# In two up stages a load of up weights is issued ahead of a load of conditioning weights, and the multiplications of the first two conditioning blocks stand in other places

## The reference, cut to what matters

```
e = silu(c @ cond_w + cond_b)
for i in range(2):
    mod = e @ ada_w[i] + ada_b[i]                 # [1024] @ [1024, 6144]
    sh1, sc1, g1, sh2, sc2, g2 = split(mod, 6)
    y = mixer[i](x * (1 + sc1) + sh1)
    x = layer_norm(ALPHA * x + (1 + g1) * y)
    gate, up = split((x * (1 + sc2) + sh2) @ ffn_up[i], 2)    # [512, 1024] @ [1024, 5632]
    y = (silu(causal_conv(gate, taps) + bias) * up) @ ffn_down[i]
    x = layer_norm(ALPHA * x + (1 + g2) * y)
# the second kind: the same pattern, with silu(c_2) @ w_ada_2 [1024] @ [1024, 6144]
```

## Time and profile before

| what | value |
|---|---|
| median of 3 runs | 2812.2 us (2811.16 to 2816.44) |
| the profiled execution, its own time | 2816.42 us |
| its span in the profile | 2814.6 us |
| mean granted clock of PE | 0.985 |
| PE busy | 2681.7 us (95%) |
| PE weight load busy | 2020.7 us (72%) |
| DVE busy | 1686.3 us (60%) |
| ACT busy | 681.3 us (24%) |
| POOL busy | 166.3 us (6%) |
| loads of the ring from the conditioning weights | 33 of 2048 KB, median 7.7 us to landing |
| loads of the ring from the up weights | 33 of 2048 KB, median 7.7 us to landing |

### The profile page before, as it was taken

One profiled execution on the slowest core, in us unless ns is written; L12 is line 12 of the kernel. 1 busy time (PEld: TensorE's weight loads), 2 busy tenths in 40 slices (PEclk: granted clock), 3 DMA queues, 4 the chain that ended last, 5 costly groups with the idle time before them and its releaser, 6 DMA issues. The chain is left out here.

```text
span 2814.6 us, 30369 instructions
## 1 busy us (share of the span) xinstructions
PE 2681.7 (95%) x11908; PEld 2020.7 (72%) x11908; DVE 1686.3 (60%) x2960; ACT 681.3 (24%) x1292; POOL 166.3 (6%) x126
## 2 busy tenths in 40 slices
PE   5999999899999999999999999998999899999999
PEld 5466666658888888888887888884445454788888
DVE  4466666557777555554657777645476483666652
ACT  0333333221111021112102111104353362322200
POOL 0001000010000011000001000001232000000000
PEclk9999999999999999999999999999999999999999
DMA  7112211214443422112122444331011300222121
GB/s 326 41 60 90 90 60 60 90 60 153 160 166 131 157 96 91 65 64 90 64 73 88 169 158 171 142 112 64 30 76 60 149 2 31 83 78 82 69 103 51
DMA packets 24493, 275.02 MB, mean 98 GB/s; under 512 B 3480, under 2 KB 4376, under 8 KB 7072
## 3 DMA queue, kind: packets, MB, share of 16 engines
q1 hardware_dynamic: 19440, 266.45, 25.4%
q10 hardware_dynamic: 4912, 6.63, 0.7%
HBM read 270.97 MB, written 2.10 MB: 97 GB/s over the span
## 5 line engine op out<-in xcount | busy, mean ns | idle before, releaser
L384 PE MATMUL bank<-HT,ring 128*128 128x256 f32 x1056 | 253.9, 387 | 9.9 <-ACT HT L794 7.4
L1102 PE MATMUL bank<-HT,ring 128*128 128x512 f32 x512 | 250.8, 599 | 5.7 <-ACT arena L1370 5.7
L384 PE MATMUL bank<-arena 128*128 128x256 f32 x1056 | 249.5, 379 | 0.0
L384 PE MATMUL bank<-arena,ring 128*128 128x256 f32 x1056 | 249.5, 379 | 0.0
L384 PEld LDWEIGHTS bank<-HT,ring 128*128 128x128 f32 x1056 | 203.7, 194 | 46.2 <-issue 15.5
L384 PEld LDWEIGHTS bank<-arena 128*128 128x128 f32 x1056 | 200.6, 190 | 27.3
L384 PEld LDWEIGHTS bank<-arena,ring 128*128 128x128 f32 x1056 | 200.6, 190 | 27.3
L466 PE MATMUL bank<-arena,ring 128*128 128x256 f32 x936 | 210.5, 384 | 8.3 <-ACT arena L538 5.6
L466 PEld LDWEIGHTS bank<-arena,ring 128*128 128x128 f32 x936 | 179.4, 192 | 36.7 <-ACT arena L538 6.8
L1030 ACT ACTIVATE arena<-bank,ffc 128x512 f32<-128x512 f32 x66 | 51.3, 777 | 498.0 <-DVE bank L942 498.0
L2368 PE MATMUL bank<-HT,ring 128*128 128x512 f32 x320 | 146.0, 593 | 3.0 <-ACT HT L834 3.0
(11 more groups left out here) (462 smaller groups left out, 4387.2 us busy)
## 6 DMA issues: line engine op xcount, KB each, us to landing
ring<-w_ada SPq DMA_DIRECT2D x33, 2048.0 KB, 7.7
ring<-w_up SPq DMA_DIRECT2D x33, 2048.0 KB, 7.7
ring<-w_down SPq DMA_DIRECT2D x24, 1408.0 KB, 6.0
ring<-w_gdn SPq DMA_DIRECT2D x8, 2048.0 KB, 8.4
ring<-w_ret_qk SPq DMA_DIRECT2D x4, 2048.0 KB, 7.8
ring<-w_ret_v SPq DMA_DIRECT2D x4, 2048.0 KB, 7.6
ring<-w_ret_g SPq DMA_DIRECT2D x4, 2048.0 KB, 7.7
ring<-w_ret_out SPq DMA_DIRECT2D x4, 2048.0 KB, 7.7
```

Of the source, the lines that this page charges most:

```text
L384: last = nc.tensor.matmul(out_, w[:, k, :], x[:, k, :], start=(first and k == 0), stop=(k == 3), skip_group_check=not first)
L1102: last = nc.tensor.matmul(B[u % 2][:, :], w[:, u, k, :], HT[:, k, :], start=(k == 0), stop=(k == KC - 1))
```

## The change

Two things change in up stages 0 and 1, and nothing in up 2. In SP's list the third load of up weights (`("up", i, 2)`) is issued ahead of block 1 of the conditioning weights. The slots stay as they were, and so does what each load waits for: the up load for DVE's last multiplication of block 0, block 1 for PE's last product with the first up load. And the first two blocks are multiplied in other steps:

| step | place | before: block, slices | after |
|---|---|---|---|
| 0 | round 0, behind t | 0: 0, 1 | 0: 0, 1 |
| 1 | round 1, ahead of t | 0: 2, 3 | 0: 2, 3, 4 |
| 2 | round 1, behind t | 0: 4, 5 | 0: 5, 6, 7 |
| 3 | round 2, ahead of t | 0: 6, 7 | none |
| 4 | round 2, behind t | 1: 0, 1 | none |
| 5 | round 3, ahead of t | 1: 2, 3 | none |
| 6 | round 3, behind t | 1: 4, 5 | 1: 0, 1, 2, 3 |
| 7 | round 4, ahead of t | 1: 6, 7 | 1: 4, 5, 6, 7 |

From step 8 on all is as before.

```diff
             def ada(j, half):

+                first_blocks = {1: (0, 0, 2), 2: (0, 2, 5), 3: (0, 5, 8), 7: (1, 0, 4), 8: (1, 4, 8)}
                 step = 2 * j + half - 1
-                if i < 2 and 0 <= step < 40:
+                if i < 2 and step < 8:
+                    if step + 1 in first_blocks:
+                        dve_ada(dve, i + 1, *first_blocks[step + 1])
+                elif i < 2 and step < 40:
                     l, k = step // 4, 2 * (step % 4)
                     dve_ada(dve, i + 1, l, k, k + 2)
@@
         def _(sp):

-            for n, key in enumerate(loads):
+            issued = list(range(len(loads)))
+            for i in range(2):
+                n = load_at[("ada", i + 1, 1)]
+                issued[n:n + 2] = [load_at[("up", i, 2)], n]
+            for n in issued:
+                key = loads[n]
```

## The result

Predicted were 2797.5 us (2793.5 to 2804.0); measured are 2799.5 us as the median of four runs (2794.5 to 2800.7), against 2811.7 for the kernel before (four runs too; the 2812.2 of the table are the median of the first three of them). The ratio is 0.9946, 95% interval 0.9934 to 0.9958. A second group of runs gave 2800.7 against 2815.1, ratio 0.9949 (0.9936 to 0.9961). The kernel is faster, by 12 to 15 us: 12.2 and 14.4 by the medians of the two groups, 15.2 and 14.4 by the ratios.

The account below looks back on a forecast made before the run. PE was taken to wait in round 3 of two up stages for DVE, held by a late weight load, then run at low clock. Losses 8.08 and 8.46 us, less 0.92 each, save 14.7: 2812.2 to 2797.5 us (2793.5 to 2804).

Parts of the forecast that it names:

- The late load: First up stage: third up-weight load issued 6.1 us earlier, so PE's last product of round 3 starts 4.40 us earlier.
- The cost at M3(1): PE's last product of round 1: an added multiplication ahead of it leaves PE 0.92 us behind its free run.
- The pair of loads: Third up load and block 1's go out together: the first lands unslowed, about 7.5 us, the second 12.4 us after issue.
- Rival A: The paired loads share the engines, so the third up load lands late, at 660.3; about 2803 us, 10%.
- Block 1 in two fours: Rounds 3 and 4: block 1's multiplications stay hidden; the later fourth up load leaves 0.3 us cover in round 5.
- Rival B: Round 5: the fourth up load comes late because block 1 moved toward it; 0.5 to 1 us per stage, 2799, 15%.
- Rival C: Behind t(3): DVE stands waiting for block 1's load, delaying round 4; slower, 2816 us if it lands after 24 us, 3%.
- Rival D: PE's gap is taken up elsewhere in the stage, so time ends within 3 us of the old; 2811, 3%.
- The clock: Low PE clock behind the round-3 gap goes with the gap; 2.18 us of the second up stage's 8.46.
- The sum: First and second up stages save 7.16 and 7.54 us, together 14.7, with nothing given back later.

Follow-up runs that it names:

- That experiment: The changed kernel with the list of loads put back as before, so only the multiplications moved: 2806.5 us, ratio to before 0.9972.
- the second profile of the changed kernel: The changed kernel run once more without edits, in another group beside the kernel before: 2800.7 us against 2815.1.
- the gap filled: The kernel before with four unread matmuls added on PE in round 3 of both up stages, ahead of the wait for t(3): 2809.6 us, ratio 0.9987.

## Why the prediction was right

*The late load.* Right (though the wait of 4.4 us that the prediction sets out from stands in the second up stage; in the first, whose timelines it reads, it is 3.41): issue 11.8 us behind M3(0) (11.7 worked out), landing after 7.6 us, no wait at line 895, M3(3) set by PE alone.

*The cost at M3(1).* Right in kind, 0.97 us behind the free run where 0.92 was put. The clock was 1.00 over 640 to 650 us, with the gap of 0.81 us in it, and 1.00 over 1524 to 1530 us in the second up stage.

*The pair of loads.* 7.6 and 12.1 us against 7.7 and 12.4 taken from the start of the program; 7.7 and 13.4 in the second up stage. Rival A is refuted: the first of a pair wasn't slowed here (7.6 and 7.7 us, where the third up load, not one of a pair, took 7.5 and 8.5 before), and each of these pairs landed in the order of its issue. So did the pairs in the other order: 7.5 us for block 1 and 12.1 for the up load, 7.6 and 13.3 in the second up stage. That experiment shows the order to be worth 2.8 and 4.5 us a stage.

*Block 1 in two fours.* Right, and its cover even thinner than said: line 895 of round 5 waits 2.98 us, t(5) starts at 681.46 and M3(5) at 682.12, which with 0.47 us for the hand-over leaves 0.2 us where 0.3 was put. PE pays nothing there; in the second profile of the changed kernel, second stage, it pays 0.06 us (12.15 us from M3(4) to M3(5)). So Rival B, at 0.5 to 1 us, did not come in the changed kernel, but did where the loads stood in the old order (0.77 us at M3(5)).

*Rival C, slower by a blocking load.* It did not come, and its mechanism is real: 12.26 us at one multiplication with the list alone changed, slower than before.

*Rival D, hidden anyway.* It did not come: behind M3(5) of the first stage the distance to M3(0) of the second is 832.9 us before and 832.8 after, so nothing of the gain was given back.

*The clock.* Right. The 8.08 us of the first stage are the 5.34 by which M3(3) is late and 2.74 of low clock: M3(3) and the product behind it take 6.19 us (667.07 to 673.26) where two products take 3.45 (2 x 1.73), and the granted clock is 0.50 of full over 667 to 671 us and 1.00 over 673.26 to 675. With the gap filled they take 3.55 us at a clock of 1.00 in both stages: 4.7 us won against 4.9.

*The sum.* 14.7 us was predicted, 14.3 measured in the stages. What is missing is 0.05 us at M3(1), 0.10 at M3(2) and 0.03 at M3(3) in each stage: I had let t(2) and PE's own run tie at 654.0, and a tie still cost 0.10 us (8.74 for 8.64). By medians the saving was 12.2 us in the first group and 14.4 in the second. The difference of 2.0 us to the predicted time is within what runs of one kernel differ by (2794.5 us with a mean clock of 0.990, 2800.7 with 0.987), and of such a difference the last section shows 6 us ahead of the first up stage.

## What to carry to other kernels

In a ring with an ordered queue of loads, as this kernel's, a load goes out when its slot is free and its place in the queue has come (17.8 us behind M3(0) with its place alone moved, 11.8 with both). Moving only its place did harm here (9.7 us), and moving only the work that frees the slot gave half; look which of the two is late, and move the work that uses the load pushed behind as well. Work of low urgency belongs where its engine idles anyway (behind t(0)), not ahead of an instruction on which PE waits. And price a gap of PE with the low clock behind it (2.7 and 2.2 us here behind gaps of 4.2 and 5.1, none behind one of 1.35), but in full only if nothing else covers those products: where they ran under another wait they cost 0.1 to 1.0 us.

## What the runs showed of the hardware

PE's clock in the stage ahead of the first up stage differs from execution to execution of the same code. Windows of before, of the first profile of the changed kernel, and of its second (the column ahead of the last two is the granted clock):

```profile
505.00:560.00 55.00, 43.75 (x229) 32.17 (x228) 28.24 (x54) 10.46 (x17) 0.50 (x1) 0.88 0.21 77
```

```profile
505.00:560.00 55.00, 42.98 (x227) 29.88 (x226) 27.06 (x54) 9.94 (x16) 0.00 (x0) 0.97 0.21 77
```

```profile
505.00:560.00 55.00, 44.14 (x214) 33.53 (x213) 26.59 (x53) 9.61 (x16) 0.00 (x0) 0.81 0.21 77
```

0.88, 0.97 and 0.81 go with M3(0) of the first up stage at 635.83, 630.93 and 637.00 us: the lower the clock there, the later the stage begins. Between the first two 0.09 of 55 us is 5.0, and 4.9 was the difference. That is a spread of 6 us in code that the change doesn't touch, where the runs of one kernel spread over 8 us (2795.9 to 2804.1), and the reason why a difference of 2 us is read better from the stage than from the time. Why the clock differs there was not tried.

The same shows at a gap that both kernels have in these profiles. PE stands idle for 1.88 us near the start of each down stage. In the second down stage the 44 rows behind it run partly at the low clock in the profile of before (0.85 over them), and at full clock (1.00) in the first profile of the changed kernel:

```profile
1790.59 11.45 PE L466 MATMUL bank<-arena,ring 128*128 128x256 f32 x44 [1.88 <-ACT arena L538]
```

```profile
1771.31 9.76 PE L466 MATMUL bank<-arena,ring 128*128 128x256 f32 x44 [1.88 <-ACT arena L538]
```

That is 1.69 us, and it is the 1.7 of the 2.6 us above. Behind the same gap in the first down stage the rows take 9.76 us in both profiles (clock 1.00), and in the third 11.45 in both (0.85). So in these two profiles a gap of 1.88 us had low clock behind it in some places and executions and not in others, and the length of the gap alone doesn't say which.
